# Expert tiles of a mixture of experts that finish their own rows: the combine stage folded into the expert stage

## The reference

```python
weight = g_top * jax.nn.softmax(e_top, axis=-1)        # two weights per token
xs = xt[tok_s]                                          # rows sorted by expert
a = jax.nn.silu(lax.ragged_dot(xs, w_gate, sizes)) * lax.ragged_dot(xs, w_up, sizes)
ys = lax.ragged_dot(a, w_down, sizes) * weight.reshape(-1)[order][:, None]
out = jnp.zeros_like(xt).at[tok_s].add(ys)
h = _layernorm(alpha * h + ffn, ln2_g[l], ln2_b[l])     # ffn is that out, alpha = 2 ** 0.25
```

## Time and profile before

| | |
|---|---|
| median of 3 runs | 4560.74 us (4558.6 to 4567.77) |
| the profiled execution | 4558.93 us |
| its span | 4557.3 us |
| PE, DVE, ACT, POOL busy | 92%, 55%, 36%, 18% of the span |
| expert tiles | 82, from 2810 us to 4300 us |
| combine | from 4301 us to the end |

### The profile page before, as it was taken

One profiled execution on the slowest core, in us unless ns is written; L12 is line 12 of the kernel. 1 busy time (PEld: TensorE's weight loads), 2 busy tenths in 40 slices (PEclk: granted clock), 3 DMA queues, 4 the chain that ended last, 5 costly groups with the idle time before them and its releaser, 6 DMA issues. The chain is left out here.

```text
span 4557.3 us, 68431 instructions
## 1 busy us (share of the span) xinstructions
PE 4181.0 (92%) x22196; PEld 3531.3 (77%) x22197; DVE 2486.4 (55%) x3696; ACT 1640.8 (36%) x2767; POOL 813.6 (18%) x741
## 2 busy tenths in 40 slices
PE   7999999999999999999999976999999999999700
PEld 7887887887887887888878865888888888888600
DVE  5555455456456446456555556554444555344388
ACT  2323323323323324224224222554444555344311
POOL 4022022022022112111211202000000000000176
PEclk9999999999999999999999988999999999999855
DMA  6233233333333333323323314774444565446387
GB/s 163 71 107 98 81 101 97 90 96 89 94 96 89 97 93 89 102 80 98 102 83 95 102 56 160 265 280 173 172 166 166 209 236 183 154 170 224 111 282 248
DMA packets 560688, 622.93 MB, mean 137 GB/s; under 512 B 90048, under 2 KB 412608, under 8 KB 560464
## 3 DMA queue, kind: packets, MB, share of 16 engines
q1 hardware_dynamic: 536992, 534.56, 36.1%
q0 software_dynamic: 23472, 85.47, 5.6%
HBM read 532.92 MB, written 87.03 MB: 136 GB/s over the span
## 5 line engine op out<-in xcount | busy, mean ns | idle before, releaser
L820 PE MATMUL bank<-hT_hi,w_hi 128*128 128x512 f32 x2176 | 864.9, 397 | 31.1 <-DVE w_lo L652 22.9
L652 DVE TENSOR_TENSOR w_lo<-raw,w_hi 128x1024 fp32r<-128x1024 f32 x400 | 598.0, 1495 | 484.6 <-ACT w_hi L511 483.4
L821 PE MATMUL bank<-hT_lo,w_hi 128*128 128x512 f32 x2176 | 850.6, 391 | 2.4 <-issue 2.4
L822 PE MATMUL bank<-hT_hi,w_lo 128*128 128x512 f32 x2176 | 849.0, 390 | 0.0
L1399 DVE TENSOR_TENSOR e_w_lo<-e_raw,e_w_hi 128x1024 fp32r<-128x1024 f32 x384 | 455.2, 1220 | 346.2 <-ACT e_w_hi L1357 343.2
L1454 PE MATMUL e_bank<-e_w_hi,e_xT_hi 128*128 128x256 f32 (+1 forms) x1968 | 627.0, 319 | 1.9 <-DVE e_xT_lo L1394 1.5
L1456 PE MATMUL e_bank<-e_w_hi,e_xT_lo 128*128 128x256 f32 (+1 forms) x1968 | 627.1, 319 | 0.0
L1455 PE MATMUL e_bank<-e_w_lo,e_xT_hi 128*128 128x256 f32 (+1 forms) x1968 | 626.9, 319 | 0.0
L820 PEld LDWEIGHTS bank<-hT_hi,w_hi 128*128 128x128 f32 x2176 | 408.9, 188 | 141.6 <-DVE w_lo L652 33.8
L822 PEld LDWEIGHTS bank<-hT_hi,w_lo 128*128 128x128 f32 x2176 | 408.9, 188 | 87.6
L821 PEld LDWEIGHTS bank<-hT_lo,w_hi 128*128 128x128 f32 x2176 | 409.2, 188 | 86.3 <-issue 5.3
(11 more groups left out here) (251 smaller groups left out, 6752.6 us busy)
## 6 DMA issues: line engine op xcount, KB each, us to landing
raw<-in_w_in_dram SPq DMA_DIRECT2D x251, 512.0 KB, 3.9
e_raw<-in_w_exp_gate_dram SPq DMA_DIRECT2D x128, 512.0 KB, 4.2
e_raw<-in_w_exp_up_dram SPq DMA_DIRECT2D x128, 512.0 KB, 9.0
e_raw<-in_w_exp_down_dram SPq DMA_DIRECT2D x128, 512.0 KB, 11.4
expert_rows<-e_y SPq DMA_DIRECT2D x82, 512.0 KB, 2.8
raw<-in_w_o_dram SPq DMA_DIRECT2D x64, 512.0 KB, 3.7
h_rows<-h_rows SPq DMA_DIRECT2D x36, 512.0 KB, 3.1
raw<-in_w_in_dram SPq DMA_DIRECT2D x64, 256.0 KB, 3.8
```

The source lines that it names most:

```text
L652: v.tensor_tensor(w_lo[:, s % 2, :], raw[:, s % RAW, :], w_hi[:, s % 2, :].bitcast(FP32), ALU.subtract).then_inc(lo_ready, 1)
L820: pe.matmul(out, hi, x_hi, start=first, stop=False)
L821: pe.matmul(out, hi, x_lo, start=False, stop=False)
L822: return pe.matmul(out, lo, x_hi, start=False, stop=last)
```

## The change

Each token's two result rows are no longer written and combined later. The mixer writes `h` twice into `h1`, which now has two copies, 4608 rows apart. The tile that has the token's lower-numbered expert gathers the row's base `h` from the first copy, adds its weighted result and writes the sum into the second copy. The tile of the other expert gathers that sum as its base, adds its own result, takes the layer norm and writes the row to `out`. Every tile issues both stores, and an index out of bounds drops the rows that do not belong. In detail:

- In **mixer** every store of `h` is issued twice.
- In **route** ACT scales each one-hot tile twice, by the row's number and by its weight (128 operations of 128x98), PE's list product has 196 columns instead of 98, and ten small DVE operations behind it make four index columns.
- In **experts**, PE makes the up product in one piece of 512 columns, and the transposes of the next rows stand ahead of the first transposes of `prod`. DVE makes three low parts of weights ahead of the product (before: two ahead of the first half and one between the halves), and closes the tile with two weighted additions, two `bn_stats` and one `bn_aggr`. ACT no longer copies a half of the result. It scales and shifts (`normalise`, 128x1024) at the head of the next tile, behind the splits of the down chunks and ahead of Silu. POOL's loop now has, for each tile: the gather of rows, the store of the sums, the deviation (three operations of 128x1), the gather of the base, the gain and the shift (two operations of 128x1024, the second into a buffer `finished`), and the store of the finished rows.
- SP has no stores in the expert stage. The function **combine** is gone.

```diff
@@ mixer, SP
-                            sp.dma_start(h1[bass.ds(b * TOK + i1 * P, P), :], h[:, i1, :]).then_inc(h1_out[i1], 16)
+                            for at in (0, TOK + S):
+                                sp.dma_start(h1[bass.ds(b * TOK + (at + i1 * P), P), :], h[:, i1, :])\
+                                  .then_inc(h1_out[i1], 16)
@@ route, ACT
+                for j in range(2 * NT):
...
+                    for q in range(2):
+                        ins = a.activation(listed[:, j % OH, q, :], hot_hi[:, j % OH, :], ACT.Copy,
+                                           scale=worth[:, j, q:q + 1])
+                    ins.then_inc(worth_made, 1)
@@ route, PE
-                    mm = pe.matmul(ranks[0][:, 0:MT], hot_lo[:, j % OH, :], hot_hi[:, j % OH, :],
+                    mm = pe.matmul(ranks[0][:, 0:2 * MT], hot_lo[:, j % OH, :],
+                                   listed[:, j % OH, :, :].rearrange("p q t -> p (q t)"),
@@ experts, POOL
+                def store_part(g):
+                    hold(po, y_taken, g * 2 + 4)
+                    po.indirect_dma_start(out=h1[:, :],
+                                          out_offset=bass.IndirectOffsetOnAxis(ap=y_at[:, 1:2], axis=0),
+                                          in_=both[:, :], in_offset=None,
+                                          bounds_check=h1.shape[0] - 1, oob_is_err=False).then_inc(part_out, 16)
...
+                def store_rows(g):
+                    hold(po, normed, g + 2)
+                    po.tensor_tensor(done[:, :], done[:, :], gain[:, :], ALU.mult).then_inc(gained, 1)
+                    hold(po, rows_out, g * 16 + 16)
+                    hold(po, gained, g * 2 + 4)
+                    po.tensor_tensor(finished[:, :], done[:, :], shift[:, :], ALU.add).then_inc(gained, 1)
...
+                with po.Fori(0, total) as g:
+                    gather_rows(g + 2)
+                    store_part(g)
+                    deviation(g)
+                    hold(po, part_out, g * 16 + 16)
+                    gather_base(g + 1)
+                    store_rows(g)
@@ experts, ACT
+                def normalise(rstds, scaled):
+                    a.wait_ge(rstd_made, rstds + 3)
+                    a.wait_ge(gained, scaled + 1)
+                    a.activation(done[:, :], both[:, :], ACT.Identity, bias=offset[:, 0:1], scale=rstd[:, 0:1])\
+                     .then_inc(normed, 1)
...
-                        a.wait_ge(gate_ready, g + 1)
-                        a.activation(act[:, :], gate_p[:, :], ACT.Silu).then_inc(act_ready, 1)
                         with a.If(g == lo):
                             a.wait_ge(y_ready, g * 2 + 2)
                             for c in range(2 * GC, CH):
                                 split_hi(e, c)
+                        normalise(g * 3, g * 2)
+                        a.wait_ge(gate_ready, g + 1)
+                        a.activation(act[:, :], gate_p[:, :], ACT.Silu).then_inc(act_ready, 1)
                         with a.If(g == swap):
@@ experts, DVE
-                        splits((0, 1), (0, 1))
+                        splits((0, 1, 2), (0, 1, 2))
                         v.wait_ge(act_ready, g + 2)
-                        for half in range(2):
-                            if half:
-                                splits((2,), (2,))
-                            v.wait_ge(up_ready, g * 2 + half + 2)
...
-                        v.tensor_copy(y[:, TOK:2 * TOK], yp[1][:, :]).then_inc(y_taken, 1)
+                        v.wait_ge(base_in, g * 16 + 16)
+                        v.wait_ge(normed, g + 1)
+                        for half in range(2):
+                            v.wait_ge(y_ready, g * 2 + 3 + half)
...
+                            v.scalar_tensor_tensor(out=both[:, part], in0=yp[half][:, :],
+                                                   scalar=slot_weight[:, bass.ds(g, 1)], in1=base[:, part],
+                                                   op0=ALU.mult, op1=ALU.add).then_inc(y_taken, 1)
@@ experts, PE
+                        transposes(g * 16 + 32)
                         product_transposed(0)
                         product_transposed(1)
-                        transposes(g * 16 + 32)
                         product_transposed(2)
```

More of the change, by code:

```diff
@@ L997, in route @@
     L = G + E
-    slot1, slot2, weight1, weight2, slot_token, bounds, slot_tiles = keep
+    row_index, slot_weight, bounds, slot_tiles = keep
     MT = slot_tiles
+    SECOND = TOK + NT * P
     with ExitStack() as ctx:
```

365 lines of the change are left out of this document (144 added, 221 removed).

## The result

| | before | after |
|---|---|---|
| time, median of the runs (lowest to highest), us | 4560.5 (4558.6 to 4567.8) | 4699.3 (4692.9 to 4700.7) |
| span of the profiled execution, us | 4557.3 | 4691.1 |
| ratio after / before | | 1.030, 95% interval 1.028 to 1.031 |

The change makes the kernel 139 us slower; 48 were forecast. The page after: its total line by engine, the granted clock over the span in 40 slices, and the row of POOL.

A forecast was written before the change was run, and what follows sets the result against it. Expert stage taken as bound by PE, combine by its chain of transfers, DVE and POOL. 4558.9 − 237 + 15 + 2 + 34 + 234 = 4607; with the profiled execution 1.8 below the median, 4609 us, range 4450 to 4715.

The forecast's parts named there:

- combine gone: End of kernel: combine's 256.4 us go, the last store lands some 19 behind the last addition; gain 237.
- PE's own order: Expert tiles: up product in one piece saves 0.32, later product transposes cost 0.73; +0.41 in 82 tiles, +34 us.
- last tiles: Last tile of 30 experts: PE waits 5.5 for the product, low clock costs 2.3; 7.8 each, +234 us (50 to 315).
- In most tiles it is hidden, as long as p is below 3.9: Expert tiles: Silu ends at p + 7.1, the product is wanted only at 11.1, so most tiles lose nothing.
- p: Start of POOL's store of sums in a tile, in us from the start of PE's gate product.
- I take 2.4: An expert's last tile: p assumed 2.4 us, between the ends 1.4 and 4.0.
- turn of 19.2: POOL's loop in the expert stage: one turn about 19.2 us against PE's tile of 18.6, POOL nearly as full as PE.
- p + 14.9 against 11.75: Last tile: product and its transpose come at p + 14.9, PE wants it at 11.75; with p = 2.4, wait 5.5 us.
- The clock was put at 2.3: Last tile: half clock behind PE's wait, worth up to 3.4 us, taken as 2.3 (bounds 0 and 3.4).
- POOL's turn bounds every tile: Rival, expert stage: landings lengthen POOL's turn to 23.5, stage 1927 instead of 1490, time 4776; decides from about 21.5; chance 0.13.
- VectorE beside GpSimd: Last tiles: VectorE's low parts are slowed beside POOL's gain and shift, to 2 to 3.5 us instead of 1.2.
- What would show it: Signs: middle tiles 18.6, last tiles 24 to 28, PEclk 0.8 to 0.95, POOL above 80% busy or waiting on landings.

The follow-up runs named there:

- run 4: The changed kernel with POOL's hold for the gathered rows moved to just ahead of the next gather: 4600 us, ratio 1.008.
- run 2: The changed kernel with POOL's gain and shift made on one column instead of 1024, so left out of the output: 4530 us, ratio 0.993.
- run 7: The kernel of run 6 with gain and shift on one column of 1024, so left out of the output: 4397 us, ratio 0.964.
- run 13: Two kernels: changed kernel with normalising, gain and shift on VectorE, 4453 us (0.976); run 12 with the changed kernel's PE order, hold late, 4452 us (0.975).
- run 5: The changed kernel with the late hold of run 4 and ScalarE's normalising behind Silu and the high parts ahead: 4443 us, ratio 0.974.
- run 9: The changed kernel with 30 more unused PE matmuls in each expert's last tile, ahead of the row transposes: 4687 us, ratio 1.027.
- run 12: The kernel of run 5 with the old PE and VectorE order, and normalising, gain and shift on VectorE: 4396 us, ratio 0.963.
- run 1: The changed kernel with ScalarE's normalising moved from ahead of Silu to behind aT's four high parts: 4643 us, ratio 1.018.
- run 3: The changed kernel with VectorE's low parts of the next expert's gate weights moved behind those of aT: 4734 us, ratio 1.038.
- run 6: The changed kernel with ScalarE's normalising behind Silu and the high parts ahead, GpSimd's holds unchanged: 4705 us, ratio 1.031.

## Why the prediction was right and wrong

Direction and mechanism held; the size did not: 139 against 48. The terms, in spans and tile lengths:

| term | forecast | measured | from |
|---|---|---|---|
| combine gone | −237 | −230 | last gate product to the end, 45.5 for 275.6 |
| router and second store | +17 | +13 | first gate product |
| PE's own order | +34 | +46 | 81 × (18.72 − 18.15) |
| last tiles | +234 | +252 | 30 × (27.13 − 18.72) |
| first and middle tiles | 0 | +50 | 29 × 0.52 + 21 × 1.93 − 80 × 0.07 |
| single tile | 0 | +3 | 8.8 now, 6.1 before |

The sum is +134, as much as the spans differ (133.8); the medians differ by 138.8.

**The step that failed** is "In most tiles it is hidden, as long as p is below 3.9", with "I take 2.4" behind it. POOL's lateness was treated as something of the last tile. But the working held p = 3.7 in a first tile (measured 3.8) and a turn of 19.2 against a tile of 18.6. A turn longer than a tile gives nothing back, so the next tile has 3.7 + 19.2 − 18.6 = 4.3, outside my own bounds of 1.4 to 4.0; with the measured turn of 20.8 it has 5.8. (The terms that the working names add up to 18.1; its 19.2 has 1.1 more that no term gives.) I let the wait of a last tile give some back, but it comes behind p, and in the next first tile VectorE's four low parts put p at 3.8 again. So a middle tile behind a first one has p = 5.1 in the mean, above the threshold, and takes 20.6. The 50 us of first and middle tiles are the largest part of the missing 90: 30 are the 19 middle tiles', half of them wait and half the low clock that 8 of them have behind it, 8 are one first tile in which POOL held 14.7 for a landing, and 6.5 are the stage's first tile, where the working had no term for down splits ahead of Silu. Runs 4, 2, 7 and 13 bear out that POOL's lateness is the cause: shortening POOL's turn took 99 to 309 us away, and the landing hold cost 99 us with the long turn and nothing with the short one. In runs 2, 7 and 13 the slow low parts went along; run 4 left them (1485 ns), and so did run 5.

**The last tile** came near, by two errors against each other. Mean Silu is at 10.7, and in the tile above Silu starts 6.6 behind p; that puts the mean p at an estimated 4.1, not 2.4. By the formula, p + 14.9 against 11.75, that is a wait of 7.2; measured 6.2, since the way from p to the transpose is a microsecond shorter: in the tile shown, p + 14.9 = 20.7 against 19.8. The clock was put at 2.3 and is worth 2.2 by run 9's working. That 7.8 a tile lay so near 8.4 is luck.

**The turn.** Forecast 19.2, measured 20.8. The hold behind the gather lasted 6.05 from its issue (3033.14 − 3027.09), where I had 4.4 for the landing. The rival "POOL's turn bounds every tile" had its threshold wrong: a turn does not start to matter at 21.5 but where it passes the tile, 18.7. It passes it in first tiles alone (20.6), so its excess is gained once in an expert and costs where p is above the threshold. POOL starts afresh with each expert, since it waits 12 us for a first tile's additions.

**VectorE beside GpSimd.** Low parts of 3184 and 3431 ns appeared as said. The first low part at 3041.36 met POOL's shift, which ran until 3043.45; the three took 5.46 instead of 3.50, 1.96 more against the 2.09 of shift that were left. By the Trainium skill (SBUF — State Buffer, SBUF: two separate sides) the port pair that the two engines share is an exclusive lock, which blocks the later one for the whole instruction; the row agrees.

**PE's order** was put at +34 and is +46 by the tiles, +56 by run 12 against 13. In the changed kernel itself, undoing it costs 47, because the order also decides what PE waits for when Silu is late. The sum had no term for that.

**Table loads.** The drain that I left out is not there: the normalising starts at 3037.23, 0.02 behind the load's end, and Silu at 3039.78, 0.01 behind. With the 1380 ns that the Trainium skill (ScalarE: Activation LUTs, What ACT_TABLE_LOAD costs) gives for it, the estimate would have been 4693, nearly the measured time, for a reason that the rows exclude.

**What would show it.** Right: combine's stretch gone, a tail of 25.6 (I had 19, with 30 as the limit), last tiles at 27.1 in the mean of a forecast 24 to 28, though some reach 30.1, the waits, the low parts, a clock of 0.92 over the stage. Wrong: middle tiles at 18.6 (20.3), and POOL above 80% busy or waiting on landings: 881 busy and some 290 of such waits in 1824.

## What to carry to other kernels

When an edit puts an in-order helper engine into a loop, work out its turn with every landing that it holds for, and compare it with the main engine's turn, for each kind of tile: here it was longer in first tiles alone, and the lateness of one turn was enough. While the turn is too long, the first wait behind it decides, and moving that wait along another engine mostly renames it (runs 1, 3 and 6). Once it is shorter, the order counts again: the late hold alone took 99 us, normalising behind Silu alone nothing, both together 256, and that was as good as giving the work to the engine with idle time beside PE (runs 5 and 13). An undone part of a change must be priced in the kernel that it is undone in, since the same order of PE cost 56 us in one and saved 47 in another.

## What the runs showed of the hardware

- A hold for an indirect gather's landing took 5.06 us behind the end of its issue, and the row names no releaser: such a hold shows as a wait for "issue".
- One VectorE operation of two SBUF inputs and 1024 columns was stretched from 1210 to 3184 ns by a GpSimd operation that had 2.09 us left.
- Of the same finishing, gain took GpSimd 2.34 to 2.42 us and shift 2.33 to 3.20, and VectorE takes 1.285 for each with a scalar folded in.
- Low clock cost far less than the time it was shown: 242 us at the lower level in last tiles, and an estimated 2.2 × 30 = 66 us of loss.
